# The second matrix of an MLP by forms instead of by pairs of tiles, and six more plain tiles ahead of the first

## The reference

```python
def finish(x, ret_y, nsa_y, w_o, ln_post_mix, ln_pre_ffn, w_up, w_down, ln_post_ffn):
    mix = jnp.concatenate([ret_y, nsa_y], -1) @ w_o
    h = x + rmsnorm(mix, ln_post_mix)
    f = jnp.square(jax.nn.relu(rmsnorm(h, ln_pre_ffn) @ w_up)) @ w_down
    return h + rmsnorm(f, ln_post_ffn)
```

## Time and profile before

| what | value |
|---|---|
| median of 3 runs | 1825.8 us (1822.82 to 1828.91) |
| the profiled execution | 1823.22 us, span 1821.5 us |
| PE busy | 1661.4 us (91%) |
| DVE busy | 1062.9 us (58%) |
| ACT busy | 693.8 us (38%) |
| POOL busy | 411.6 us (23%) |
| DMA | 201.94 MB, mean 111 GB/s |

### The profile page before, as it was taken

The page is one execution under the profiler, slowest core; times in us unless marked ns, Lnnn a source line. Parts: engine busy times, 40 slices in busy tenths (PEclk is TensorE's granted clock), DMA queues, the critical chain, the costliest instruction groups (busy, mean ns, idle before and its releaser), DMA issues. The chain is left out here.

```text
span 1821.5 us, 31492 instructions
## 1 busy us (share of the span) xinstructions
PE 1661.4 (91%) x12256; PEld 1471.2 (81%) x12256; DVE 1062.9 (58%) x1767; ACT 693.8 (38%) x1274; POOL 411.6 (23%) x415
## 2 busy tenths in 40 slices
PE   5999999995999679999989986899999798989997
PEld 4989988995874655565559876899999798989997
DVE  5556442130126367777866656767776847584666
ACT  5212322210011156666646555333333424242443
POOL 1000000013434200000000103422222527484311
PEclk9999999997999789999999998999999899999999
DMA  8111011144967400000035552234344615150665
GB/s 292 47 48 48 25 47 42 47 110 132 250 168 199 130 12 1 1 1 1 1 108 171 159 156 92 88 124 160 130 146 150 252 47 210 47 209 27 215 176 164
DMA packets 207493, 201.94 MB, mean 111 GB/s; under 512 B 15213, under 2 KB 181954, under 8 KB 203762
## 3 DMA queue, kind: packets, MB, share of 16 engines
q1 hardware_dynamic: 171586, 152.23, 26.7%
q0 software_dynamic: 12720, 37.21, 6.7%
q10 hardware_dynamic: 23040, 10.50, 2.2%
HBM read 161.18 MB, written 42.89 MB: 112 GB/s over the span
## 5 line engine op out<-in xcount | busy, mean ns | idle before, releaser
L2416 PE MATMUL psum<-right_hi,left_hi 128*128 128x258 f32 x1120 | 323.1, 289 | 30.3 <-DVE down_u L2795 16.8
L2416 PE MATMUL psum<-right_hi,left_lo 128*128 128x258 f32 x1120 | 321.8, 287 | 0.0
L2416 PE MATMUL psum<-right_lo,left_hi 128*128 128x258 f32 x1120 | 321.3, 287 | 0.0
L2416 PEld LDWEIGHTS psum<-right_hi,left_hi 128*128 128x128 f32 x1120 | 217.5, 194 | 32.7 <-DVE down_u L2795 17.6
L2416 PEld LDWEIGHTS psum<-right_lo,left_hi 128*128 128x128 f32 x1120 | 217.5, 194 | 0.0
L2416 PEld LDWEIGHTS psum<-right_hi,left_lo 128*128 128x128 f32 x1120 | 217.1, 194 | 0.0
L235 PE MATMUL psum<-act_hi,whi 128*128 128x344 f32 x648 | 213.3, 329 | 4.0 <-DVE act_lo L408 4.0
L235 PE MATMUL psum<-act_hi,wlo 128*128 128x344 f32 x648 | 206.9, 319 | 0.0
L235 PE MATMUL psum<-act_lo,whi 128*128 128x344 f32 x648 | 206.8, 319 | 0.0
L235 PEld LDWEIGHTS psum<-act_hi,whi 128*128 128x128 f32 x648 | 121.8, 188 | 11.5 <-DVE act_lo L408 4.5
L235 PEld LDWEIGHTS psum<-act_lo,whi 128*128 128x128 f32 x648 | 121.8, 188 | 0.4
(11 more groups left out here) (449 smaller groups left out, 3808.9 us busy)
## 6 DMA issues: line engine op xcount, KB each, us to landing
hidden_forms<-pair_out SPq DMA_DIRECT2D x84, 258.0 KB, 2.5
right_raw<-hidden_forms SPq DMA_DIRECT2D x21, 1032.0 KB, 7.7
pair_raw<-in_w_up SPq DMA_DIRECT2D x14, 1024.0 KB, 5.6
wraw<-in_w_in SPq DMA_DIRECT2D x27, 512.0 KB, 3.8
pair_raw<-in_w_down SPq DMA_DIRECT2D x12, 1024.0 KB, 5.2
...
```

What stands on the lines that cost most here:

```text
L2416: last = pe.matmul(ps[:, BANKS[pos] + e, 0:HT // 2], wt[:, kt, :], xt[:, kt, cols], start=(pos < 3 and kt == 0 and i == 0), stop=(kt == 3 ...
```

## The change

- **Head**: six blocks of outputs of w_up are made plainly instead of four: 42 plain tiles instead of 36, and 13 pairs in the first matrix instead of 14. `scale_x` is spread over tiles 16 to 27 and 32 to 35. The differences of x are made in halves behind tiles 33 to 38, all on DVE, and the first pair's weight sums too. From tile 26 on, DVE evacuates a tile ahead of `reduce_lo`.
- **Second matrix**: within a slab the work goes form by form: four products (the four pairs of output tiles) with one right form, each in two banks of its own, then the next form. Forms that add to the same output follow each other. Four places hold the right forms in turn, so a form is loaded some twelve products before its use. Each product is added to y in SBUF straight from PSUM on DVE (`add_to_y`); the first form of a slab goes to three of the four quarters, on ACT for slab 0 (`first_into_y`), on DVE in slabs 1 and 2 with a second operation of 1032 columns. Weights lie as four 512 x 512 blocks of 1 MB in five places, and their sums are made once for a slab, in halves of 1024 columns, on DVE (`block_sum`). POOL does nothing here any more; the low parts of forms are two halves on DVE (`form_lo_of`).
- The last part's two first right operands have places of their own and are loaded during slab 1.

```diff
-UP_PAIRS = SLABS * PAIRS + 2
-MIX_PAIRS = UP_PAIRS + SLABS * PAIRS
-PRODUCTS = FORMS * MIX_PAIRS
+HEAD_TILES = 6
+UP_PAIRS = SLABS * PAIRS + 1
+UP = FORMS * UP_PAIRS
+DOWN = FORMS * PAIRS
+PRODUCTS = UP + DOWN * SLABS
...
+DOWN_FORMS = (0, 4, 1, 3, 5, 2, 6)
+A11, A12, A21, A22, SPARE = range(5)
+DOWN_LEFT = (A11, A12, A11, A21, A22, SPARE, A12)
...
-    return tiles + [("up", n, c) for c in range(3) for n in range(4)]
+    return tiles + [("up", n, c) for c in range(3) for n in range(HEAD_TILES)]
...
+def form_steps():
+    out = []
+    for j in range(FORMS * SLABS):
+        load = UP - FORMS + (2, 3, 4, 6)[j] if j < 4 else UP + PAIRS * (j - 3)
+        high = load + (2, 3, 4, 4)[j] if j < 4 else load + 3
+        out.append((j // FORMS, DOWN_FORMS[j % FORMS], j % 4, load, high, high + 1, high + 2))
+    for part, place, load in ((0, 4, UP + 41), (1, 5, UP + 49), (2, 1, UP + 72), (3, 2, UP + 76)):
+        out.append((SLABS, part, place, load, load + 3, load + 4, load + 5))
+    return sorted(out, key=lambda step: step[3])
...
+        BLOCK_LOADS = [(0, A11, UP - FORMS - 3), (0, A21, UP - FORMS + 1), (0, A12, UP - FORMS + 3), (0, A22, UP - FORMS + 4)]
+        for k in range(1, SLABS):
+            BLOCK_LOADS += [(k, role, UP + DOWN * (k - 1) + d) for role, d in ((A12, 14), (A11, 15), (A21, 18), (A22, 22))]
...
+        X_SCALES = ((0, 1), (4, 5), (2, 3), (6, 7))
+        X_PARTS = {33: ((1, 0),), 34: ((0, 0),), 35: ((1, 1),), 36: ((0, 1), (2, 0)), 37: ((2, 1),), 38: ((3, 0), (3, 1))}
+        X_DIFFS_FOR = (4, 3, 6, 8)
+        BLOCK_SUMS = [(k, n, UP + DOWN * k + ((-1, 0, 1, 2, 3, 4, 12, 13) if k == 0 else (-3, -2, -1, 0, 1, 2, 12, 13))[n])
+                      for k in range(SLABS) for n in range(8)]
...
+        def y_reads(at):
+            d = at - UP
+            return max(d - PAIRS, 0) + max(0, min(d - DOWN, PAIRS)) + max(0, min(d - 2 * DOWN, PAIRS))
...
+                if place < 4:
+                    sp.wait_ge(product_done, at)
...
-            for at in range(PRODUCTS):
-                g, pos = divmod(at, FORMS)
-                adds = g >= UP_PAIRS + PAIRS
-                if g + 1 < MIX_PAIRS:
-                    if pos == 0:
-                        left_sum(g + 1, 0)
-                        left_sum(g + 1, 1)
-                    elif pos in (2, 3):
-                        left_sum(g + 1, pos)
-                if adds and pos in (1, 2, 5):
-                    add_to_y(g, (1, 2, 5).index(pos))
-                if at in (1, 3):
-                    x_lo_part(2 + at // 2)
-                for n, (_, _, _, _, split) in enumerate(loads):
-                    if split == at:
-                        form_lo_part(n)
-            pool.wait_ge(y_pool, 3 * PAIRS * (SLABS - 1))
+            pool.wait_ge(left_sums, 4)
+            for g in range(1, UP_PAIRS):
+                for i in range(4):
+                    left_sum(g, i)
 ...
+            def bank_wait(at):
+                if at >= UP:
+                    _, i, n = down_place(at)
+                    if at < UP + PAIRS:
+                        pe.wait_ge(psum_read, 6 * UP_PAIRS - (2, 1, 0, 0)[n])
+                    elif at < UP + 2 * PAIRS:
+                        pe.wait_ge(y_first, 2 * (n + 1))
+                    else:
+                        pe.wait_ge(y_read, y_reads(at - PAIRS + 1))
+                    return
...
+            def first_into_y(at):
+                n = down_place(at)[2]
+                act.wait_ge(product_done, at + 1)
+                src = banks(first_bank(at))
+                act.activation(y_part(0, n, 1), src, ACT.Copy).then_inc(y_first, 1)
+                act.activation(y[1][:, n, :].rearrange("p (h a n) -> p h a n", h=2, a=2), src.unsqueeze(1).broadcast_to([P, 2, 2, HT // 2]),
+                               ACT.Copy).then_inc(y_first, 1)
...
-                if NO <= u < 4 * KT:
-                    scale_x(2 * (u - NO))
-                    scale_x(2 * (u - NO) + 1)
-                if u in (4 * KT, 4 * KT + 1):
-                    for n in range(4):
-                        scale_x(16 + 4 * (u - 4 * KT) + n)
+                if 2 * KT <= u < NO:
+                    scale_x(u - 2 * KT)
+                if NO <= u < NO + 4:
+                    scale_x(KT + 2 * (u - NO))
+                    scale_x(KT + 2 * (u - NO) + 1)
+                if 4 * KT <= u < 4 * KT + 4:
+                    for kt in X_SCALES[u - 4 * KT]:
+                        scale_x(2 * KT + kt)
+                if u in (38, 40):
+                    x_hi_of((u - 38) // 2)
...
+            def form_lo_of(j, q):
+                place, kts = steps[j][2], slice(2 * q, 2 * q + 2)
+                dve.wait_ge(f_form_hi, j + 1)
+                dve.tensor_tensor(right_lo[place][:, kts, :], right_f[place][:, kts, :], right_hi[place][:, kts, :].bitcast(F32),
                                   ALU.subtract).then_inc(f_form_lo, 1)
...
+            def block_sum(slab, n):
+                i, q = divmod(n, 2)
+                kts = slice(2 * q, 2 * q + 2)
+                at = weight_places(slab)
+                a11, a12, a21, a22, s1 = (blocks[at[role]][:, kts, :] for role in (A11, A12, A21, A22, SPARE))
+                base, first = 8 * slab, UP + DOWN * slab
+                if n == 0:
+                    for role in (A21, A22):
+                        dve.wait_ge(block_loaded[at[role]], 16 * block_loads(slab, role))
+                    dve.wait_ge(form_lo, first)
+                if n == 2:
+                    dve.wait_ge(block_loaded[at[A11]], 16 * block_loads(slab, A11))
+                if n == 6:
+                    dve.wait_ge(block_loaded[at[A12]], 16 * block_loads(slab, A12))
+                if i:
+                    dve.wait_ge(block_sums, base + (None, 1, 3, 5)[i] + q)
+                if i == 2:
+                    dve.wait_ge(form_lo, first + PAIRS)
+                if i == 3:
+                    dve.wait_ge(form_lo, first + 2 * PAIRS)
+                out, p, sub, op = ((s1, a21, a22, ALU.add), (a21, a11, a21, ALU.subtract), (a11, s1, a11, ALU.subtract),
+                                   (a12, a12, a11, ALU.subtract))[i]
+                dve.tensor_tensor(out, p, sub, op).then_inc(block_sums, 1)
...
+            def add_to_y(at):
+                slab, i, n = down_place(at)
+                src = banks(first_bank(at))
+                dve.wait_ge(product_done, at + 1)
+                if slab == 0 and 0 < i:
+                    dve.wait_ge(y_first, 2 * (n + 1))
+                if at - UP > 2 * PAIRS:
+                    dve.wait_ge(y_read, y_reads(at - PAIRS + 1))
+                if i == 0:
+                    if slab == 0:
+                        return
+                    to = y_part(0, n, 1)
+                    dve.tensor_tensor(to, to, src, ALU.add).then_inc(y_read, 1)
+                    to = y[1][:, n, :].rearrange("p (h a n) -> p h a n", h=2, a=2)
+                    dve.tensor_tensor(to, to, src.unsqueeze(1).broadcast_to([P, 2, 2, HT // 2]), ALU.add).then_inc(y_read, 1)
+                    return
+                to = y_part(*((None, (0, n, 0), (0, n, 1), (1, n, 1), (1, n, 0), (1, n, 1), (0, n, 1))[i]))
+                if slab == 0 and i == 1:
+                    dve.tensor_copy(to, src).then_inc(y_read, 1)
+                else:
+                    dve.tensor_tensor(to, to, src, ALU.add).then_inc(y_read, 1)
...
-                if u in head_ends:
+                early = u in head_ends or u > NO + 1
+                if early:
                     evacuate(u - 1)
                 if u and u + 1 < NU:
                     reduce_lo(u + 1)
                 k, j = place_of(u)
                 if k is not None:
                     behind_chunk(k, j)
-                if u and u not in head_ends:
+                if u and not early:
                     evacuate(u - 1)
                 if u < 8:
...
+                for n, q in X_PARTS.get(u, ()):
+                    x_difference(n, q)
+                if u == 39:
+                    first_sums()
+                if u == 40:
+                    x_lo_of(0, 0)
+                    x_lo_of(0, 1)
+                    left_lo_of(0)
                 if u == NU - 1:
...
+                for slab, n, when in BLOCK_SUMS:
+                    if when == at:
+                        block_sum(slab, n)
                 if at + LEAD < PRODUCTS:
                     left_lo_of(at + LEAD)
```

544 lines of the change are left out of this document (258 added, 286 removed).

## The result

The changed kernel takes 1780.1 us (median of 4 runs, 1776.8 to 1781.8) against 1824.7 (4 runs): ratio 0.9755, interval 0.9732 to 0.9777. Its profiled execution took 1776.8 us with a span of 1775.2, 46.3 less than the span in the earlier trace rows; the sum of the terms was 52.3.

The account below looks back on a forecast made before the run. TensorE, busy 91% of 1821.5 us, was taken as the bound, through matmul count and waits or slow clock. Terms -1 + 14 - 12.4 - 20.3 - 30.9 - 1.7 = -52.3 gave 1770.9, put at 1772, range 1758 to 1796.

Parts of the forecast that it names:

- the steady part of the second matrix: Second matrix with POOL silent: DVE needs 8.4 us per four products against PE's 11.6; no wait, 243.9 us for 84 products.
- slower than before: Rival: DVE's lengthening comes from something that stays, DMA or ACT; a group costs 14.8 us, time 1839; chance 0.04.
- The head's cost of ten tiles: Tiles 32 to 41: ten tiles at 3.8 us and 2 us of sums and spreads, 40 us against 26.0, +14.
- the pause at product 91: Sign at the second matrix's start: one pause of about 6 us, released by `right_lo` with the load of `down_weights` behind it.
- DVE paces in part: Rival in the second matrix: DVE's rows at full length with gaps lose 1 us in each of 21 groups, 1793; chance 0.10.
- the short bank waits: Rival: slab-start pauses reappear as PSUM bank waits, 0.5 us for each of 84 products; 1803; chance 0.04.
- Second matrix, start: DVE waits for A22, landing at 21 us: pause 6.7, with slow clock 8.4; 252.3 against 283.2, -30.9.
- the bound of 11: Upper bound for the pause at the second matrix's start, in us, if A22 lands in 25.
- The second estimate: Second matrix's start, by the skill's about 436 GB/s: A22 in at 18.5 us, pause 4.2 instead of 6.7.
- First products: First three products: DVE's work to 9.5 us plus 0.7 for POOL's sums, 10.2 instead of 22.6, -12.4.
- Last part: Its first matmul no longer waits for POOL's `right_lo`; the slow clock in the last window goes, -1.7; 24 tiles unchanged.
- Head: Tiles 16 to 31: moved scalings lose 2.4, the later tiles save 3.5 with evacuation ahead of `reduce_lo`; net -1.

Follow-up runs that it names:

- experiment 1: Changed kernel with block A22 asked for together with A21, at product 85 instead of 88: 1769.4 us, ratio 0.969 to the kernel before.
- experiments 6 and 7: Changed kernel plus 70 or 140 unread 128x512 products on POOL in the second matrix: 1790.2 us (ratio 0.9809) and 1834.1 us (1.0048).
- experiment 8: Changed kernel with the second matrix's block sums on POOL instead of DVE, A22 asked for where it was: 1781.6 us, ratio 0.9769.
- experiment 5: Kernel before the change, with POOL's quarter of each form's low part done by DVE: 1815.5 us against 1827.0, ratio 0.995.
- 12: Changed kernel with the first block sum, which waits for A22, moved from DVE's step 90 to step 91: 1768.6 us, ratio 0.9685.
- Experiments 3 and 11: 3: changed kernel, last plain tile's store ahead of second pair's load, 1773.8 us. 11: also A22 asked for earlier, second pair's weight sums on DVE, 1760.5 us.
- Experiment 4: Changed kernel with the head's old order (scalings in tiles 24 to 31, evacuation behind `reduce_lo`): 1785.0 us, ratio 0.9772.

## Why the prediction was right, and where it was off

The forecast was 1772 with a range of 1758 to 1796; 1780.1 lies inside, 8 us above the forecast. Read against the spans, term by term (predicted, measured):

| stretch | predicted us | measured us | off by |
|---|---|---|---|
| earlier stages and tiles 0 to 15 | 0 | +1.0 | +1.0 |
| tiles 16 to 31 | -1 | -3.5 (+2.4, -5.9) | -2.5 |
| tiles 32 to 41 | 40 | 39.3 | -0.7 |
| first three products | 10.2 | 13.5 | +3.3 |
| 88 products to product 91 | 256.1 | 255.9 | -0.2 |
| second matrix with its pause | 252.3 | 254.6 | +2.3 |
| last part | 113.6 | 116.4 | +2.8 |
| sum | -52.3 | -46.3 | +6.0 |

**Right.** The central claim was that the steady part of the second matrix would have no wait, and it has none. That it took 244.0 us where 243.9 was written is luck: 2.3 us of it are the slow clock behind the pause, and without them the 84 products take 241.7 (experiment 1). The pace of 2.904 us had been read from a window that begins behind a 3.64 us pause, at a granted clock of 0.50 for 3.4 us; from 1154.0 on the kernel before does 2246 matmuls in 269.0 us at full clock, 2.874 for a product. DVE had 9.3 us of work for a group of four products (194.7 in 21 groups) and not 8.4, against PE's 11.5.

The reason given, that DVE's rows are short where POOL is silent, is shown by experiments 6 and 7: they put POOL's work back, with ACT as busy as before (98.5 us), and the rows lengthen. At 140 operations DVE has 14.0 us of work for each of 21 groups, and the second matrix takes 299.2 us, 14.2 a group; the rival "slower than before" had put the turning point at 14.1. Its 1839 was for 14.8 a group, so the measured 1834 doesn't confirm that number, and its cause, something that stays, is refuted. The Trainium skill ("SBUF — State Buffer", the section on SBUF's two sides) names an exclusive lock on a port pair held for the whole instruction; the pair of rows at 1500 and the burst of experiment 8 agree with it.

What isn't shown is how much of the gain in this stretch is POOL's silence and how much the new order, in which splits and sums are spread over the slab. The kernel before had 163.1 us of POOL here. With 107.7 the changed kernel still is 1.9% faster than it, of 2.5; only with 251.6 is the gain gone. No run has the new order with the old work of POOL, or the old order with POOL silent (experiment 5 takes away a part of POOL's work and gives 0.5%).

The head's cost of ten tiles, and the place of the pause at product 91, behind `right_lo` and the load of `down_weights`, came as written. Neither "DVE paces in part" nor the short bank waits came: PE has no other wait.

**Second matrix, start**: mechanism right, size off. The pause was 10.6 us, not 6.7, near the bound of 11. The term that was mis-sized is A22's landing: 24.8 us, not 21. The amount was about right (7.37 MB asked for up to A22, written 7.6). But 21 stands for a pace of 0.36 MB/us, and 94% of A22 had moved only at 22.6 us, 0.33 MB/us; and the tail of A22, another 2.1 us up to its last signal, was left out. The second estimate there has A22 in at 18.5 us, but 7.6 MB at the rate that it names are 17.4. The step also treated the pause as the load's price. Experiments 8 and 12 show that it is a price of order: PE needs nothing of A22 until product 99. Two smaller errors nearly cancel: the slow clock cost 2.3 instead of 1.7, and the 84 products at full clock 241.7 instead of 243.9.

**First products**: the step took DVE's own work as the limit and 0.7 us for POOL. The parts that it lists make 5.6 us, and it doesn't say what the rest of its 8.9 is; `take_u2` began 12.9 us after product 0. The store's wait was left out although SP's order was there to read, and POOL's sums cost more, about 2.2 us on two rows. Behind the pause of 4.8 us PE ran at half speed (granted clock 0.50 from 1148.3 to 1151.7). Experiments 3 and 11 remove the two causes one after the other.

**Last part**: a miscount. In the kernel before, 18 matmuls (2.8 us) of the first tile of the last part ran ahead of its pause, inside the window of the second matrix (2033 matmuls where 84 products have 2016). The first term took them as saved, and this one didn't charge them.

**Head**: the moved scalings cost what was worked out, and the two edits in tiles 24 to 31 gave 5.9 instead of 3.5. Experiment 4 shows that the edits, and not noise, made most of it.
